# Decoding tokens taken out of the dense expert product: their v rows gathered by indirect DMAs and summed on VectorE

## The reference

```python
def block(xt):
    q = (xt @ peer_w_q).reshape(PEER_BLOCK, PEER_HEADS, 2, D_KEY_HALF).astype(f32)
    s1 = jnp.einsum('thd,nd->thn', q[:, :, 0], keys1)
    s2 = jnp.einsum('thd,nd->thn', q[:, :, 1], keys2)
    v1, i1 = lax.top_k(s1, PEER_TOPK)
    v2, i2 = lax.top_k(s2, PEER_TOPK)
    ...
    best_s, pos = lax.top_k(cand_s, PEER_TOPK)
    idx = jnp.take_along_axis(cand_i, pos, axis=-1)
    gate = jax.nn.softmax(best_s, axis=-1)
    act = jax.nn.gelu(jnp.einsum('thkd,td->thk', peer_u[idx], xt).astype(f32), approximate=False)
    return jnp.einsum('thk,thkd->td', (gate * act).astype(peer_v.dtype), peer_v[idx])
```

## Time and profile before

| | us |
|---|---|
| median of three runs | 1413.51 (1412.66 to 1414.91) |
| the profiled execution | 1415.16 |
| its span | 1413.4 |
| PE busy | 1376.3 (97%) |
| PEld busy | 1313.6 (93%) |
| DVE busy | 991.8 (70%) |
| ACT busy | 684.1 (48%) |
| POOL busy | 506.5 (36%) |

### The profile page before, as it was taken

The page is one execution under the profiler, slowest core; times in us unless marked ns, Lnnn a source line. Parts: engine busy times, 40 slices in busy tenths (PEclk is TensorE's granted clock), DMA queues, the critical chain, the costliest instruction groups (busy, mean ns, idle before and its releaser), DMA issues.

```text
span 1413.4 us, 34628 instructions
## 1 busy us (share of the span) xinstructions
PE 1376.3 (97%) x11325; PEld 1313.6 (93%) x11325; DVE 991.8 (70%) x2303; ACT 684.1 (48%) x1454; POOL 506.5 (36%) x672
## 2 busy tenths in 40 slices
PE   8999999989999999999999999999999999999996
PEld 6977787788999999999999999999999999999995
DVE  5348777767699995888888888856555555555556
ACT  4665544324445666444444444444444444444444
POOL 5000022302649998766666666652000000000000
PEclk9999999999999999999999999999999999999998
DMA  4343110013414545544444444445555555554553
GB/s 139 120 141 93 50 57 3 3 39 135 135 62 141 141 140 142 134 120 119 119 119 121 122 120 119 119 135 150 149 150 149 150 148 149 148 148 148 148 149 96
DMA packets 85288, 168.69 MB, mean 119 GB/s; under 512 B 9914, under 2 KB 11466, under 8 KB 85034
## 3 DMA queue, kind: packets, MB, share of 16 engines
q1 hardware_dynamic: 85226, 167.84, 40.8%
HBM read 164.80 MB, written 2.97 MB: 119 GB/s over the span
## 4 chain that ended last, share of the span: by engine, by line
PE 84%; POOL 5%; DVE 4%; issue 4%; ACT 2%; DMA 1%; SPq 0%; POOLq 0%; DVEq 0%; ACTq 0%
PE PS L1055 23%; PE PS L1057 22%; PE PS L1056 22%; POOL hlo L642 5%; PE PS L1488 5%; PE PS L1151 1%; PE PS L1335 1%; PE PS L1337 1%; PE PS L1320 1%; PE PS L1443 1%; PE PS L1050 1%; PE PS L1062 1%; DVE wlo L1570 1%; DVE XF L1570 0%; DVE states L1570 0%
## 5 line engine op out<-in xcount | busy, mean ns | idle before, releaser
L642 POOL TENSOR_TENSOR hlo<-hraw,hhiq 128x256 fp32r<-128x256 f32 x512 | 397.8, 787 | 144.8 <-ACT hhiq L690 142.6
L1055 PE MATMUL PS<-H1h,hhiq 128*128 128x320 f32 x1024 | 343.8, 336 | 3.4 <-POOL hlo L642 3.1
L690 ACT ACTIVATE hhiq<-hraw 128x256 fp32r<-128x256 f32 x508 | 210.9, 417 | 258.1 <-PE PS L1057 230.8
L1057 PE MATMUL PS<-H1h,hlo 128*128 128x320 f32 x1024 | 315.4, 308 | 0.0
L1056 PE MATMUL PS<-H1l,hhiq 128*128 128x320 f32 x1024 | 315.1, 308 | 0.0
L1057 PE MATMUL PS<-Wh,hlo 128*128 128x320 f32 x1016 | 314.0, 309 | 0.0
L1055 PEld LDWEIGHTS PS<-H1h,hhiq 128*128 128x128 f32 x1024 | 193.6, 189 | 9.3 <-POOL hlo L642 6.8
L1056 PEld LDWEIGHTS PS<-H1l,hhiq 128*128 128x128 f32 x1024 | 193.4, 189 | 0.0
L1057 PEld LDWEIGHTS PS<-H1h,hlo 128*128 128x128 f32 x1024 | 192.2, 188 | 0.0
L1057 PEld LDWEIGHTS PS<-Wh,hlo 128*128 128x128 f32 x1016 | 190.7, 188 | 0.0
L2011 DVE TENSOR_SCALAR oh<-iotak,pair 128x128 f32<-128x128 f32 x320 | 128.2, 401 | 48.4 <-PE PS L1488 43.8
(11 more groups left out here) (342 smaller groups left out, 2644.8 us busy)
## 6 DMA issues: line engine op xcount, KB each, us to landing
hraw<-in_uT SPq DMA_DIRECT2D x256, 256.0 KB, 2.6
hraw<-in_vE SPq DMA_DIRECT2D x254, 256.0 KB, 2.6
wraw<-in_wbig SPq DMA_DIRECT2D x50, 512.0 KB, 3.9
xin<-in_xT SPq DMA_DIRECT2D x4, 336.0 KB, 4.2
out_yT<-XF SPq DMA_DIRECT2D x8, 160.0 KB
ckx<-in_ckT SPq DMA_DIRECT2D x2, 512.0 KB, 6.9
vs<-in_cv SPq DMA_DIRECT2D x1, 768.0 KB, 8.2
out_ko<-kx SPq DMA_DIRECT2D x1, 672.0 KB
```

Source lines behind the costliest of these rows:

```text
L642: nc.gpsimd.tensor_tensor(hlo[q // 2 % 4][:, cols_], hraw[q // 2 % 4][:, cols_], hhiq[q % 4][:].bitcast(F32), ALU.subtract).then_inc(s_hlo ...
L690: return nc.scalar.activation(out, in_, f, **kw)
L1055: mm(out, whi_, xhi, start=start, stop=False)
L1057: return mm(out, wlo_, xhi, start=False, stop=stop)
```

## The change

The 64 decoding tokens leave the grid, W and the down products, which shrink to TM = 256 columns; up keeps 320. NGR falls from 80 to 64 groups and `W` to 128 x 128 x 256.

In their place: the third score tile is made of the 64 decoding tokens twice, in both partition halves, so that the lower half can serve heads 0 to 3 and the upper heads 4 to 7: 64 picks for each of 128 rows. After routing, VectorE makes three index tiles. In up, ScalarE applies Gelu to the 64 columns apart (`gd`) and stores them from its own queue to a scratch tensor `gsc` in HBM, 32 KB for each step. When all are stored, GpSimd fetches the 64 x 128 activations by 64 indirect DMAs of 128 single elements, and then, for each of 64 picks, the v rows of 128 token halves by two indirect DMAs of 128 rows of 2 KB (`rows_of`, 512 KB together, ring `vr` of four). VectorE multiplies by gate x activation and adds into `Ys`, eight picks for every ten steps from step 48 on. In the last step TensorE folds the two halves of Ys into columns 256 to 319 of each bank, with a float32 matmul against `fold`. From step 2 on, Wl is made by GpSimd (`w_low`) and no longer by VectorE.

```diff
+TM = TQ - DEC
+NGR = TM // 4
+VFROM, VPER = 48, 10
+LATER = {VFROM + 1 + (m // 4) * 5 + m % 4: (m + 4,) for m in range(60)}
...
+            def rows_of(n):
+                for x in range(2):
+                    nc.gpsimd.indirect_dma_start(vr[n % 4][:, 512 * x:512 * x + 512], None, vE.rearrange("a p c -> (a p) c"),
+                                                 bass.IndirectOffsetOnAxis(vix[x][:, n:n + 1], 0)).then_inc(s_vr[n % 4], 16)
+
+            pool.wait_ge(s_ys, 1)
+            own(nc.gpsimd.memset(fold[:], 0.0))
+            for c in (0, HD):
+                select(fold[:], [[-1, HD]], ALU.not_equal, -c, 1, 1.0)
+            nc.gpsimd.sem_inc(s_rconst, 1)
+            for x in range(4):
+                pool.wait_ge(s_row[x], GELUS_OUT)
+            def w_low(e):
+                pool.wait_ge(s_wh, e + 1)
+                nc.gpsimd.tensor_tensor(Wl[e % 2][:], W[:, e, :], Wh[e % 2][:].bitcast(F32), ALU.subtract).then_inc(s_wl, 1)
+
+            for n in range(HD):
+                nc.gpsimd.indirect_dma_start(acts[:, n:n + 1], None, gsc.rearrange("e i (t o) -> (e i t) o", o=1),
+                                             bass.IndirectOffsetOnAxis(aix[:, n:n + 1], 0)).then_inc(s_vr[0], 16)
+                if n % 2:
+                    w_low(2 + n // 2)
+            for n in range(4):
+                rows_of(n)
+                w_low(34 + n)
...
             for k in range(KT):
+                w_low(38 + k)
                 pool.wait_ge(s_down, 8 + 2 * k)
...
+            w_low(46)
+            w_low(47)
+            for e in range(VFROM, NI):
+                w_low(e)
+                for m in LATER.get(e, ()):
+                    pool.wait_ge(s_ys, m - 1)
+                    rows_of(m)
...
-                up_ = PS[:, slot % 4, 0:TQ]
-                A(W[:, bass.ds(e, 1), :].rearrange("p a t -> p (a t)") if direct else up_, up_, ACT.Gelu).then_inc(s_gelu, 1)
+                up_ = PS[:, slot % 4, 0:TM]
+                A(W[:, bass.ds(e, 1), :].rearrange("p a t -> p (a t)") if direct else up_, up_, ACT.Gelu)
+                if isinstance(e, int) and e >= 4:
+                    act.wait_ge(s_row[slot % 4], X_DONE + e // 4 * 16)
+                elif not isinstance(e, int):
+                    act.wait_ge(s_row[slot % 4], e * 4 + (X_DONE - 4 * (slot % 4)))
+                A(gd[:, slot % 4, :], PS[:, slot % 4, TM:TQ], ACT.Gelu).then_inc(s_gelu, 1)
+                if not isinstance(e, int) or e > 0:
+                    keep_gelu(e - 1, slot - 1)
+
+            def keep_gelu(e, slot):
+
+                act.wait_ge(s_gelu, e + 1)
+                nc.scalar.dma_start(gsc[bass.ds(e, 1)].rearrange("a p t -> (a p) t"), gd[:, slot % 4, :]).then_inc(s_row[slot % 4], 16)
...
-                for u, t0 in enumerate((0, P, TQ - P)):
+                for u in range(3):
                     for x in range(2):
                         out = flat(PS, 512 * (2 + 2 * (h % 3)) + (2 * u + x) * NK, NK)
-                        ins = mm(out, QT[:, 2 * h + x, t0:t0 + P], kst[:, x, :], start=True, stop=True)
+                        if u < 2:
+                            mm(out, QT[:, 2 * h + x, P * u:P * u + P], kst[:, x, :], start=True, stop=True)
+                        else:
+                            for c in CHUNKS:
+                                ins = mm(out[c, :], QT[:, 2 * h + x, TM:TQ], kst[:, x, :], start=True, stop=True)
...
-                        ins = three(PS[:, 4 * b + kk, 0:TQ], hhv[2 * s + b][:, P * kk:P * kk + P], lo_[:, P * kk:P * kk + P],
+                        ins = three(PS[:, 4 * b + kk, 0:TM], hhv[2 * s + b][:, P * kk:P * kk + P], lo_[:, P * kk:P * kk + P],
                                     Wh[s][:], Wl[s][:], start, stop)
                         if stop:
-                            ins.then_inc(s_fin, 1)
+                            j = 4 * b + kk
+                            mm(PS[:, j, TM:TQ], Ys[:, P * j:P * j + P], fold[:], start=True, stop=True).then_inc(s_fin, 1)
...
+            def ranks(by):
+                for c, hs in sides:
+                    ins = v.scalar_tensor_tensor(rank[c, :], sel[c, 5, hs, :].rearrange("p h k -> p (h k)"), by,
+                                                 sel[c, 2, hs, :].rearrange("p h k -> p (h k)"), ALU.mult, ALU.add)
+                own(ins)
...
             def down(e, s):
-                down_w(e, s)
                 for b in range(2):
                     down_v(e, b, s, hlo[2 - 2 * s + b], hraw[2 - 2 * s + b])
...
-            with dve.Fori(1, NI // 2) as k:
+            v.memset(Ys[:], 0.0).then_inc(s_ys, 1)
+            with dve.Fori(1, VFROM // 2) as k:
                 for e in range(2):
                     down(k * 2 + e, e)
+            dve.wait_ge(s_vr[0], ACTS_IN[0] + 32)
+            own(tt(coef[:], acts[:], gat[:], ALU.mult))
+            with dve.Fori(1, (NI - VFROM) // VPER + 1) as k:
+                y = 0
+                for x in range(VPER):
+                    down(k * VPER + (VFROM - VPER + x), x % 2)
+                    if x % 5 < 4:
+                        dve.wait_ge(s_vr[y % 4], k * 64 + (ACTS_IN[y % 4] + 32 * (y // 4) - 32))
+                        dve.wait_ge(s_ys, k * 8 + (y - 6))
+                        v.scalar_tensor_tensor(Ys[:], vr[y % 4][:], coef[:, bass.ds(k * 8 + (y - 8), 1)], Ys[:], ALU.mult,
+                                               ALU.add).then_inc(s_ys, 1)
+                        y += 1
```

More of the change, by code:

```diff
@@ L232, in build @@
         unit = tail.put("unit", [P, 1])
+        tok = tail.put("tok", [P, 1])
         hhv = [at(f"hhv{i}", [P, 512], hole_at + 2048 * i, F32R) for i in range(2)] + hhi
@@ L238, in build @@
         wsplit = Region(pairs_at, SBUF_END)
-        Wh = [wsplit.put(f"Wh{i}", [P, TQ], F32R) for i in range(2)]
-        Wl = [wsplit.put(f"Wl{i}", [P, TQ], F32R) for i in range(2)]
-        W = at("W", [P, NI, TQ], BASE)
+        Wh = [wsplit.put(f"Wh{i}", [P, TM], F32R) for i in range(2)]
+        Wl = [wsplit.put(f"Wl{i}", [P, TM], F32R) for i in range(2)]
+        W = at("W", [P, NI, TM], BASE)
         picked = Region(BASE + 99872, BASE + 134464)
@@ L250, in build @@
         cand = ranked.put("cand", [P, 3, 16, 16])
+        few = Region(BASE + NK * TM * 4, BASE + 134464)
+        rank = few.put("rank", [P, HD])
+        aix = few.put("aix", [P, HD], U32)
+        vix = [few.put(f"vix{i}", [P, HD], U32) for i in range(2)]
+        gat = few.put("gat", [P, HD])
+        acts = few.put("acts", [P, HD])
+        coef = few.put("coef", [P, HD])
+        fold = few.put("fold", [P, HD])
+        mid = Region(BASE + 134464, BASE + 154944)
+        gd = mid.put("gd", [P, 4, DEC])
+        Ys = mid.put("Ys", [P, D])
+        vr = [mid.put(f"vr{i}", [P, D]) for i in range(3)]
+        vr.append(at("vr3", [P, D], BASE + 154944))
+        gsc = nc.dram_tensor("gsc", (NI, P, DEC), F32, kind="Internal").ap()
         routing = Region(hole_at, TAIL)
@@ L423, in build @@
         s_vhi, s_vlo, s_wh, s_wl, s_down = (sem(x) for x in ("s_vhi", "s_vlo", "s_wh", "s_wl", "s_down"))
+        s_row = s_x
+        X_DONE, GELUS_OUT = 16, 16 + 16 * NI // 4
+        s_vr, ACTS_IN = [sem(f"s_vr{i}") for i in range(4)], (16 * HD, 0, 0, 0)
+        s_ys = sem("s_ys")
         s_sum, s_yf = sem("s_sum"), sem("s_yf")
@@ L653, in _ @@
             own(nc.gpsimd.memset(unit[:], 1.0))
+            for c in CHUNKS:
+                own(nc.gpsimd.iota(tok[c, :], pattern=[[0, 1]], base=0, channel_multiplier=1,
+                                   allow_small_or_imprecise_dtypes=True))
             nc.gpsimd.sem_inc(s_rconst, 1)
@@ L975, in _ @@
             up_rest(0)
-            with act.Fori(1, GATED) as k:
+            up_rest(1, blank=True)
+            with act.Fori(2, GATED) as k:
                 up_rest(k, blank=True)
@@ L1016, in _ @@
             gelu(NI - 1, NI - 1, False)
+            keep_gelu(NI - 1, NI - 1)
             for b in range(2):
@@ L1505, in _ @@
                     pe.wait_ge(s_routed, 2)
-                for tt in range(3):
+                for tt in range(2):
                     ins = nc.tensor.transpose(PS[:, 4 + x, P * tt:P * tt + P],
@@ L1544, in _ @@
                     down(k * 2 + e, e, False, False)
-            for e in range(NI - 2, NI):
-                down(e, e % 2, False, e == NI - 1)
+            down(NI - 2, 0, False, False)
+            pe.wait_ge(s_rconst, 2)
+            pe.wait_ge(s_ys, HD + 2)
+            down(NI - 1, 1, False, True)
             pe.wait_ge(s_onesg, 2)
@@ L1993, in _ @@
             v.tensor_copy(gsum[:], b3[:, :, 0]).then_inc(s_routed, 1)
+            sides = [(c, slice(4 * i, 4 * i + 4)) for i, c in enumerate(CHUNKS)]
+            def ranks(by):
[3 more added lines that the diff above has]
+                own(ins)
+            ranks(float(NK))
+            own(v.tensor_scalar(rank[:], rank[:], float(DEC), tok[:, 0:1], ALU.mult, ALU.add))
+            own(v.tensor_copy(aix[:], rank[:]))
+            ranks(2.0 * NK)
```

(3 more changed lines are left out.)

16 lines of the change are left out of this document (9 added, 7 removed).

## The result

The changed kernel takes 1424.83 us (median of 4 runs, 1422.33 to 1428.78) against 1413.38 (4 runs, 1412.66 to 1414.91) of the kernel before on the same chip: ratio 1.0076 [1.0065, 1.0088], slower by 0.8%. The profiled execution took 1422.33, its span is 1420.6. The forecast was 1371, faster by 3%. The time lies in the range and the sign is wrong.

What follows compares the result with a forecast made beforehand. TensorE, busy 97%, bounds the kernel before; down 415 against 450.3 us (-35) and up and before -8 turn the profiled 1415.2 into 1372, less 1.7 for the median: 1371 said. Range for 8 in 10: 1335 to 1440.

Steps and rivals of the forecast that it cites:

- TensorE's matmul: In down, a matmul of 256 columns takes 117.5 ns, where one of 320 took 146.6.
- The fourth rival: In down, matmuls of 256 columns stay at 146 ns, weights being the floor: 1407 us, chance 0.04.
- the ceiling of the gain: Down if TensorE alone bounds it: 2.82 us a step, 361 us, 89 less.
- Up: Up and the part before it: 16 groups fewer give -13.6 us, scores +3, ScalarE +3; together -8.
- GpSimd's gather: Steps 2 to 33 of down: two element gathers, a w_low and 0.1 of waits on GpSimd bound a step at 3.29 us.
- c: Time one indirect DMA holds GpSimd: estimated 1.2 us, between 0.33 and 2.6; the forecast's most sensitive number.
- the rival of dear gathers: GpSimd's stream bounds down everywhere, slower from 1.52 us an indirect DMA on; 1467 us at 1.8; chance 0.22.
- The ring: Four v load tiles in down, each back after its half plus 4.4 us: 2.91 us a step, 2.95 with waits.
- From step 48: Steps 48 to 127 of down, with sums and row gathers: 3.25 us a step, 260 us together.
- loads held up by the gathers: From step 48 of down, v loads land 0.5 us later beside gathers, adding 0.17 us a step.
- rival of the transfers: Gathers hold up each v load 1.3 us: 3.56 us a step from step 48, 1396 us, chance 0.10.
- the two signs of a wrong forecast: Either an indirect DMA holds GpSimd above 1.5 us, or TensorE is not idle in down at all.

Runs made afterwards that it cites:

- eight tiles: Changed kernel with eight v tiles in the load ring instead of four: 1372.21 us; with Wl on VectorE too (the 852-record reading) 1325.18 us.
- the run without gathers: Changed kernel without both kinds of indirect DMA and without the sums, Wl made by VectorE again: 1341.81 us, ratio 0.9484.
- thin rows: Changed kernel with each v row gather fetching 64 bytes a row instead of 2 KB, as many gathers, full sums: 1406.95 us, ratio 0.9937.

## Why the prediction was wrong, step by step

**TensorE's matmul: right.** A run of them in after's timeline, with lines left out; from the first to the last 14 matmuls start:

```profile
934.42 0.28 PE L1127 MATMUL PS<-Wl,hhv 128*128 128x256 f32 x1
...
936.02 0.28 PE L1126 MATMUL PS<-Wh,hhi 128*128 128x256 f32 x1
```

1.60 / 14 = 114 ns, where 117.5 was said; over whole steps, where TensorE has no gap, it is 117.4 (100 us over 852 records with eight tiles). The fourth rival (no shorter matmul) is out, and the ceiling of the gain was as large as thought, even a little larger.

**Up: right in sum, better by 4.** Up as a whole is 13.1 shorter (13.6 said for the sixteen groups). Up starts 0.6 us later, so the scores cost 0.6 of the 3 put on them, which is the end of the bounds where half-height matmuls run side by side. ScalarE's longer Gelu and its issue cost nothing that shows (3 said). So up and before gave 12.5 where 8 was said.

**GpSimd's gather: mechanism right, term too small.** c was 1.2 and the instruction is 1.15. But each also has an issue gap of 0.16 to 0.30, for which the sum had 0.1 for the whole step, and w_low takes 0.88 where 0.79 was said. The price that counts is about 1.38, and with w_low 2 x 1.38 + 0.88 = 3.64 for 3.29. That is 32 x 0.34 = 11 us. The break-even of 1.52 was not reached, and yet the kernel is slower: the rival of dear gathers gave the sign by a mechanism that holds only in steps 2 to 33.

The Trainium skill (DMA: Bandwidth & Descriptors, Anatomy of one DMA — SWDGE (gpsimd) path) had spoken for a small cost of emitting descriptors. A gather of 128 elements or rows holds GpSimd for 1.15 us here, whether an element or a row is fetched, so the measurement decides against reading it so in a loop of 3 us. The number of indices was not varied, so what of the 1.15 is fixed stays open.

**The ring.** Alone it takes 3.00 and not 2.91 (the run without gathers). Steps 34 to 47, where 2.95 was said, took 45.1 us in TensorE's timeline (its first matmul of step 34 starts at 1056.61, of step 48 at 1101.69), 3.22 each: 4 us. I had let GpSimd's w_low cost nothing there, with rows and H1s on its queue. That this is the reason is not shown. Counted the same way these steps take 3.17 with Wl on VectorE and 3.29 with thin rows, no real change, but 2.96 with eight tiles and Wl still on GpSimd. So it was the ring's depth here too; what lengthened its round stays open. The row below, of the run with Wl on VectorE, reads 24 x 49 / 381 = 3.09, but it holds steps 35 to 50, behind that run's stall and with sums only in the last three.

```profile
1051.00:1100.00 49.00, 48.43 (x381) 46.96 (x381) 28.52 (x49) 23.99 (x46) 3.98 (x3) 0.98 0.62 172
```

**From step 48: the step that failed.** It carries 80 x (3.75 - 3.25) = 40 us of down's 55. (Step 48 starts at 1101.69 and down ends at 1403.3; less 1.8 for the fold that is 299.8 over 80 steps.) What it had wrong is what a late load costs in a ring of four. Its terms against the runs:

| | said | shown |
|---|---|---|
| ring and sums, loads in time | 3.06 | 3.20 (thin rows, and Wl's 0.42 on VectorE) |
| loads held up by the gathers | 0.17 | 0.56 (that kernel against Wl on VectorE) |
| w_low and VectorE delay each other, w_low late | 0.02 to 0.2, 0.02 in the sum | 0.33 alone (3.53 - 3.20), nothing on top of the loads |

The largest miss is the second line, and two errors multiply in it. The loads were put 0.5 us later and came 0.9 to 1.2 later. And the prediction had itself worked out that every microsecond in the ring costs 0.5 a step, then used a third, since it hung the delay on another chain through the sum. (Its own rival of the transfers used the half.) 0.56 over the 1.1 us between the landings (3.9 with Wl on VectorE, 2.8 with thin rows) is the half again. The rival of the transfers had 1.3 us and 1396; it named the mechanism and gave it a chance of 0.10.

The third line was priced as small because VectorE had begun by the time Wh came. The timeline of after has a place where it is not so; both engines, one view:

```profile
1207.91 0.69 DVE L1648 TENSOR_TENSOR hlo<-hraw,hhv 128x512 fp32r<-128x512 f32 x1 [1.25 <-ACT hhv L747]
1208.52 2.09 DVE L2196 SCALAR_TENSOR_TENSOR Ys<-vr,coef,Ys 128x1024 f32<-128x1024 f32 x1
1208.77 0.75 POOL L706 TENSOR_TENSOR Wl<-W,Wh 128x256 fp32r<-128x256 f32 x1
...
1211.27 0.38 PE L1126 MATMUL PS<-Wh,hhi 128*128 128x256 f32 x1 [0.94 <-DVE hlo L1648]
```

The sum is begun when a w_low starts under it, and instead of some 1.3 us it takes 2.09; the next subtraction stands behind it, and TensorE idles 0.94. The 1.23 us said for a sum is near what it takes undisturbed; the mean of after is 1.52 (L2196, above), of the version with eight tiles and Wl on VectorE 1.28. The Trainium skill (SBUF — State Buffer, Who interferes with whom) has this exclusion, and the 2.09 and the 7.49 us agree with it. By its rule whoever issues first keeps the other out; here the one that is lengthened is VectorE, which by the profile's starts had begun first in both, and starts on GpSimd are rough, so the order is not shown.

**The sum.** The start of down +1, steps 2 to 33 +11, 34 to 47 +4, from 48 +40: some 55 of down, against 4.5 gained in up and 0.4 behind down. 1372 + 50.3 is the 1422.3 of the profiled execution. That the time fell inside the range is no merit of the mechanism: the range reached to 1440 for dear gathers (c = 1.66), and they were not dear. The forecast's chance for slower, 0.22, rested on one number, c. With the late loads at 3.76 and GpSimd's part at 3.53, both above the 3.52 of a step before, either alone was enough, in a ring of four, to lose nearly all of the gain; with eight tiles GpSimd's part is 3.26 and the kernel gains.

**What would show it.** The signs named were the right ones: the matmul's distance, a mean of GpSimd's indirect DMA, Wl as TensorE's wait up to step 33 and hlo from 48, landings above 2.6 late only (from step 48, not from 34: from 1051 to 1100 us the median is still 2.6). The three step lengths were off. Of the two signs of a wrong forecast neither came (c was 1.15, and TensorE was idle in down), and yet it was wrong: neither bears on the price of a late load.

## What to carry to other kernels

Before an engine that bounds is made faster, work out how long each buffer of the ring behind it is on its way, and give the ring room for that way at its loaded length, not at its idle one. The same change that cost 11 us with four tiles gained 41 with eight, and 93 with the other engine's bound taken away as well and its instructions spread. (Eight tiles in the kernel before were not run; its TensorE has no gap in down that they could close.) Where one fix brings nothing, try it together with the next one: two bounds of like height hide each other, and four runs in a table tell them apart.

## What the hardware showed that was not expected

An indirect DMA of 128 indices holds GpSimd 0.94 to 1.84 us, and 0.16 to 0.30 of issue, whether it fetches 4 bytes, 64 bytes or 2 KB a row (means 1.15, 1.23, 1.15 us). The bytes cost the DMA engines, not GpSimd. The mean of the 2 KB row gathers does move from version to version: 0.97 with eight tiles and Wl on VectorE, 1.26 with eight tiles and Wl on GpSimd, 1.19 with four tiles and Wl on VectorE. What moves it was not found.

The DMA engines carried 332 to 335 GB/s in a mix of 2 KB packets with a share of 0.95, at landings of 5.3 us for a load that alone lands in 2.6; at 250 GB/s it is 3.6 to 4.0. So 250 GB/s at a landing half as long again is no sign that the engines are full.

Back-to-back GpSimd instructions can hold a VectorE instruction for their whole run: 7.49 us beside eight H1s for a subtraction of 0.42; one H1s alone had made one of 0.69 last 1.39. Between the H1s VectorE never got its turn. That spreading them takes the stall away was shown; how the turn is given was not looked at.
